# Second block's mixer: attention in small pieces between weight chunks, heads in pairs, four banks in place of two

## The chip, the cores and the metric

The program runs on one core of a Trainium2 chip. The metric is the device time of one execution, in microseconds (us), and each kernel is told by the median of its runs. A profile is one execution of it, recorded instruction by instruction. TensorE (PE) does the matmuls, VectorE (DVE), ScalarE (ACT) and GpSimd (POOL) the rest, and SyncE (SP) issues the loads of the weights.

## The reference

Two transformer blocks of two layers each, on 256 tokens of width 1024, in float32. The change touches the mixer of the second block, which is computed twice (once per layer):

```
(qa, ckv, iq, ik, iw, qs, ks, vs, cb, cc, ch, ga, gb, gc) = split(x @ w_in)
# branch a: 8 heads; an indexer picks the 64 best keys of each query, latent attention on them
score = sum_h iw_h * relu(iq_h . ik);  idx = top_k(causal(score), 64)
logits = (q_h @ w_uk_h) . ckv + bias(t - s);  p = softmax(logits on idx);  y_a = (p @ ckv) @ w_uv
# branch b: stick breaking, 8 heads of width 64
z = qs . ks / 8 ;  A[t,s] = sig(z_ts) * prod_{s<j<t} (1 - sig(z_tj)), s < t ;  y_b = A @ vs
# branch c
y_c = cb * causal_depthwise_conv3(cc * ch)
merged = sum_j sigmoid(gate_j) * (y_j @ w_branch_j);   return merged @ w_out
```

## The kernel before

All weights, some 455 MB, stream once through the core in a fixed list of chunks. A WIDE chunk is 128 x 2048 values, a HALF chunk 128 x 1024. Each goes through a ring of four slots (`RING = 4`): SP loads `raw`, ACT rounds it into `w_hi` (`split_hi`, L434), DVE subtracts to get the rest, `w_lo` (`split_lo`, L438), and PE multiplies both parts with both parts of the activations: three matmuls for one (`mm3`, `tokens`), 48 matmuls of 256 columns for a WIDE chunk in `two_tiles` (L500 to L502), 24 for a HALF one. ACT and DVE split chunk c+4 when PE has finished chunk c; `ahead.to(n)` means "split up to chunk n now", at that place of the engine's own order. The results of a chunk go to one of four PSUM banks (`acc`), and ACT or DVE must empty the bank before PE's fourth chunk from there. The other four banks are `stat`, `bc` and the two of `aux`.

Every engine's order is written by hand, as one program per engine with semaphores between them; a waiting instruction holds up all that stands behind it on its engine. In a mixer of the second block (`mix2`, twice) the chunks are numbered from `c0`: c0 to c0+4 give vs, iq, ckv, ik and iw, c0+5 to c0+16 twelve WIDE chunks, then twelve pairs of a `gate` (WIDE) and a `branch` (HALF) up to c0+40, then w_out. Between them PE does the attention, in float32, and mostly in the two banks of `aux`:

- behind c0+6: the eight heads' indexer products (`dots`, L818 and L819), each bank emptied by an ACT relu (L1275) before PE may use it again, then the turning of ckv (L825);
- behind c0+7: `q @ w_uk` (L836), in two rounds, the second after ACT has copied the first (L1289);
- behind c0+14: six blocks of logits (L849, L853). DVE takes each with its bias (L1866, L1870). Before that DVE has done the eight rounds of the top 64 (L1846, L1848), on both blocks of queries in turn, and POOL has masked the penalty;
- behind c0+17 (gate 0): 24 transposes of the probabilities (`turn`, L865), after maxima, exponentials and division of the block (DVE L1877 to L1887, ACT L1308); then p @ ckv (L924, L928), later times w_uv (L934);
- from gate 2 on, the eight stick-breaking heads, one per chunk: `z` (L876, L877) in `aux`, then ACT |z|, exp and ln (L1352 to L1356), DVE (L1925), POOL's mask (L2041), then `arg` in `stat` or `bc`: the same product once more (L889, L890) and three matmuls with triangles onto it (L891 to L893), ACT exp (L1362), POOL's mask, and `weigh` (L900, L901), which ACT and DVE split into `branches` (L1367, L1930).

Of the kernel before, what the change touches and what calls it, by code (L numbers as in the profile page):

```python
# [6 lines left out]
F32 = mybir.dt.float32  # L7
# [97 lines left out]
def pack2(i, out):  # L105

    w = {k[:-2]: v for k, v in i.items() if k.endswith("_2")}
    for l in range(LAYERS):
        for f in range(2):
            if f:  # L110
# [8 lines left out]
                out[WIDE] += [moving(vs), moving(iq), wide(qa), conv, wide(qs), wide(ks),  # L119
# [128 lines left out]
def program(nc, t):  # L248
# [11 lines left out]
    with ExitStack() as ctx:  # L260
# [52 lines left out]
        flips = (stat, bc)  # L313

# [58 lines left out]
        R = lambda n: gates[:, 12 + 2 * (n % 2):14 + 2 * (n % 2)].rearrange("p a b -> p (a b)")[:, 0:384]  # L373
# [6 lines left out]
        AW = lambda n: gates[:, 16 + 2 * (n % 2):18 + 2 * (n % 2)].rearrange("p a b -> p (a b)")[:, 0:384]  # L380
        GT = lambda n: tmp[:, 16 + 2 * (n % 2):18 + 2 * (n % 2)]
# [115 lines left out]
        def _(pe):  # L497
# [295 lines left out]
            def mix2(s, l):  # L793
# [10 lines left out]
                two_tiles(c0 + 5, t0 + 6, 8, x_hi, x_lo)  # L804

                pe.wait_ge(e["ik_rows"], 4 * (l + 1))
                pe.wait_ge(e["iq_ready"], 2 * (l + 1))
                for tt in range(2):
                    last = nc.tensor.transpose(aux[:, 0, tt * P:(tt + 1) * P], IKT[:, tt].rearrange("p d c -> p (d c)"), ident[:, :])
                last.then_inc(e["ik_turned"], 1)  # L810
                two_tiles(c0 + 6, t0 + 7, 8, x_hi, x_lo)

                pe.wait_ge(e["ik_ready"], l + 1)
                for h in range(8):
                    if h >= 2:
                        pe.wait_ge(e["dots_relu"], 8 * l + h - 1)
                    r = slice(64 * (h % 2), 64 * (h % 2) + 64)
                    nc.tensor.matmul(aux[:, h % 2, 0:P], IQ[r, h // 2, 0:P], IK[r, 0:P], start=True, stop=True)  # L818
                    nc.tensor.matmul(aux[:, h % 2, P:3 * P], IQ[r, h // 2, P:S], IK[r, :], start=True,  # L819
                                     stop=True).then_inc(e["dots_done"], 1)  # L820

                pe.wait_ge(e["ck_ready"], l + 1)
# [4 lines left out]
                two_tiles(c0 + 7, t0 + 8, 8, x_hi, x_lo)  # L827
                for q in (5, 6):
                    emptied(pe, t0 + q + 1)
                pe.wait_ge(e["ckf_ready"], l + 1)  # L830
                for h in range(8):
                    r = slice(64 * (h % 2), 64 * (h % 2) + 64)
                    if h in (4, 5):
                        pe.wait_ge(e["lat_ready"], 4 * l + h - 3)

                    last = nc.tensor.matmul(aux[:, h % 2, (h // 2 % 2) * S:(h // 2 % 2 + 1) * S], UK[r, (h // 2) * P:(h // 2 + 1) * P],  # L836
                                            QA[r, h // 2], start=True, stop=True)
                    if h % 4 >= 2:
                        last.then_inc(e["lat_done"], 1)
                for j in range(8, 15):  # L840
                    two_tiles(c0 + j, t0 + j + 1, 8, x_hi, x_lo)

                pe.wait_ge(e["lat_ready"], 4 * (l + 1))
                for n in range(6):
                    if n >= 2:
                        pe.wait_ge(e["log_taken"], 6 * l + n - 1)
                    if n < 4:
                        for hh in range(2):
                            last = nc.tensor.matmul(aux[:, n % 2, hh * S:(hh + 1) * S], QL[:, 2 * n + hh, P:S], CKF[:, :],  # L849
                                                    start=True, stop=True)  # L850
                    else:
                        for hh in range(4):
                            last = nc.tensor.matmul(aux[:, n % 2, hh * P:(hh + 1) * P], QL[:, 4 * (n - 4) + hh, 0:P],  # L853
                                                    CKF[:, 0:P], start=True, stop=True)
                    last.then_inc(e["log_done"], 1)
                for j in (15, 16):
                    two_tiles(c0 + j, t0 + j + 1, 8, x_hi, x_lo)

                def turn(n):

                    pe.wait_ge(e["turned_copied" if n >= 2 else "log_taken"], 6 * l + n - 1 if n >= 2 else 6 * (l + 1))
# [6 lines left out]
                def z(h):  # L868
                    if h == 0:
                        for q in range(13, 17):  # L870
                            emptied(pe, t0 + q + 1)
                        pe.wait_ge(e["ya_parts"], 2 * (l + 1))
                    if h >= 2:
                        pe.wait_ge(e["sp_ready"], 8 * l + h - 1)
                    r = slice(64 * (h % 2), 64 * (h % 2) + 64)
                    nc.tensor.matmul(aux[:, h % 2, 0:S], KS[r, h // 2, 0:P], QS[r, h // 2, :], start=True, stop=True)  # L876
                    nc.tensor.matmul(aux[:, h % 2, S:384], KS[r, h // 2, P:S], QS[r, h // 2, P:S], start=True,  # L877
                                     stop=True).then_inc(e["z_done"], 1)

                def arg(h):  # L880

                    out = (stat, bc)[h % 2]
                    if h >= 2:
                        pe.wait_ge(e["yb_parts"], 8 * l + h - 1)
# [1249 lines left out]
```

## Time and profile before

| what | us |
|---|---|
| runs | 2693.92, 2693.96, 2688.5 |
| median | 2693.92 |
| the profiled execution | 2687.6 |
| its span (first to last instruction) | 2685.9 |
| PE busy | 2559.0 (95%) |
| DVE busy | 1520.0 (57%) |
| ACT busy | 1240.6 (46%) |
| one mixer, from the start of c0+5 to the first matmuls of c0+41 | 263.74 |
| the same in the second layer | 263.71 |

The profiled execution lies 6.3 us under the median. 1.7 us lie around its span. In the trace a float32 matmul has two records, so that "x8" of such a line are four matmuls of the program; a weight chunk's matmuls (L500 to L502) and a transpose have one each. A matmul's duration runs until its results are there, and the next one starts before that: what a piece costs is read from start to start.

### The profile page before, as it was taken

The page shows a single profiled execution, that of the slowest core. Times are in us where ns is not written, and L with a number is a line of the kernel's source. Part 1 is how long each engine was busy: PE and PEld are TensorE (multiplying, and loading weights), DVE is VectorE, ACT ScalarE, POOL GpSimd, SP SyncE. Part 2 cuts the span into 40 slices and gives each one's busy share as a digit, 9 for nine tenths or more (in the row PEclk, how much of TensorE's full clock was granted, in tenths as well). Part 3 has the DMA queues.
Part 4 walks back from the last instruction along what each step waited for, and adds up shares of the span by engine and source line. Part 5 has one row for each costly group of instructions (what it writes and reads, how often), then busy time and mean ns, then how long its engine had stood idle before and what let it go on. Part 6 is the DMA issues. An engine that isn't in the chain of part 4 may idle for free.

```text
span 2685.9 us, 33010 instructions
## 1 busy us (share of the span) xinstructions
PE 2559.0 (95%) x13936; PEld 2203.0 (82%) x13936; DVE 1520.0 (57%) x1532; ACT 1240.6 (46%) x1354; POOL 88.1 (3%) x137
## 2 busy tenths in 40 slices
PE   7999899999998999999999899899999998999998
PEld 6888888888888878887889788788888887798787
DVE  5556865555468765464556437654655564365654
ACT  4435544444456544344353654444444434744442
POOL 0000300000002100000000000000000000100000
PEclk9999999999999999999999899999999988999999
DMA  7545345455453355565443235454555532353542
GB/s 271 183 166 212 118 149 196 173 182 211 173 200 136 143 179 182 185 221 190 176 169 116 92 136 189 165 205 173 206 187 184 188 111 79 111 188 141 217 175 94
DMA packets 68561, 454.88 MB, mean 169 GB/s; under 512 B 7568, under 2 KB 9744, under 8 KB 17600
## 3 DMA queue, kind: packets, MB, share of 16 engines
q1 hardware_dynamic: 62784, 432.18, 44.4%
q0 software_dynamic: 3552, 17.98, 1.9%
q10 hardware_dynamic: 2080, 2.62, 0.3%
q8 instruction: 111, 1.82, 0.3%
q14 instruction: 34, 0.28, 0.0%
HBM read 450.13 MB, written 2.62 MB: 169 GB/s over the span
## 4 chain that ended last, share of the span: by engine, by line
PE 81%; DVE 8%; ACT 7%; issue 4%; DMA 0%; POOL 0%; DVEq 0%; SPq 0%; ACTq 0%; POOLq 0%
PE acc L532 20%; PE acc L534 20%; PE acc L533 20%; PE acc L500 5%; PE acc L502 5%; PE acc L501 5%; ACT w_hi L434 4%; DVE w_lo L438 2%; PE aux L601 1%; DVE tmp L1680 1%; PE stat L548 0%; DVE tmp L1691 0%; PE bc L548 0%; DMA raw<-in_w 0%; PE aux L1005 0%
## 5 line engine op out<-in xcount | busy, mean ns | idle before, releaser
L438 DVE TENSOR_TENSOR w_lo<-raw,w_hi 128x2048 fp32r<-128x2048 f32 (+1 forms) x430 | 940.5, 2190 | 854.5 <-ACT w_hi L434 851.9
L434 ACT ACTIVATE w_hi<-raw 128x2048 fp32r<-128x2048 f32 (+1 forms) x430 | 786.2, 1832 | 636.0 <-PE acc L534 580.0
L532 PE MATMUL acc<-w_hi,x_hi 128*128 128x512 f32 (+1 forms) x1664 | 653.6, 393 | 20.8 <-DVE x_lo L1492 11.7
L534 PE MATMUL acc<-w_lo,x_hi 128*128 128x512 f32 (+1 forms) x1664 | 647.3, 389 | 0.0
L533 PE MATMUL acc<-w_hi,x_lo 128*128 128x512 f32 (+1 forms) x1664 | 646.8, 389 | 0.0
L532 PEld LDWEIGHTS acc<-w_hi,x_hi 128*128 128x128 f32 x1664 | 314.6, 189 | 88.7 <-issue 14.3
L534 PEld LDWEIGHTS acc<-w_lo,x_hi 128*128 128x128 f32 x1664 | 314.2, 189 | 65.2
L533 PEld LDWEIGHTS acc<-w_hi,x_lo 128*128 128x128 f32 x1664 | 314.8, 189 | 62.2
L500 PE MATMUL acc<-x_hi,w_hi 128*128 128x256 f32 x1216 | 352.4, 290 | 0.0
L501 PE MATMUL acc<-x_lo,w_hi 128*128 128x256 f32 x1216 | 347.4, 286 | 0.0
L502 PE MATMUL acc<-x_hi,w_lo 128*128 128x256 f32 x1216 | 347.0, 285 | 0.0
L532 PE MATMUL acc<-w_hi,h_parts 128*128 128x512 f32 x704 | 275.2, 391 | 0.0
L534 PE MATMUL acc<-w_lo,h_parts 128*128 128x512 f32 x704 | 274.1, 389 | 0.0
L533 PE MATMUL acc<-w_hi,h_parts 128*128 128x512 f32 x704 | 274.0, 389 | 0.0
L500 PEld LDWEIGHTS acc<-x_hi,w_hi 128*128 128x128 f32 x1216 | 237.1, 195 | 3.5 <-issue 1.9
L501 PEld LDWEIGHTS acc<-x_lo,w_hi 128*128 128x128 f32 x1216 | 236.9, 195 | 0.7 <-issue 0.5
L502 PEld LDWEIGHTS acc<-x_hi,w_lo 128*128 128x128 f32 x1216 | 236.7, 195 | 0.0
L534 PEld LDWEIGHTS acc<-w_lo,h_parts 128*128 128x128 f32 x704 | 132.2, 188 | 27.5
L532 PEld LDWEIGHTS acc<-w_hi,h_parts 128*128 128x128 f32 x704 | 132.2, 188 | 27.0
L533 PEld LDWEIGHTS acc<-w_hi,h_parts 128*128 128x128 f32 x704 | 132.2, 188 | 27.0
L500 PE MATMUL acc<-branches,w_hi 128*128 128x256 f32 x384 | 110.9, 289 | 0.0
L1075 ACT ACTIVATE tmp<-acc 128x512 f32<-128x512 f32 (+1 forms) x96 | 54.0, 563 | 121.7 <-PE acc L534 121.6
(335 smaller groups left out, 2377.6 us busy)
## 6 DMA issues: line engine op xcount, KB each, us to landing
raw<-in_w SPq DMA_DIRECT2D x388, 1024.0 KB, 4.8
raw<-in_w SPq DMA_DIRECT2D x40, 512.0 KB, 3.2
tmp<-in_norm_gb POOLq DMA_DIRECT2D x8, 1024.0 KB, 5.2
tmp<-in_norm_gb POOLq DMA_DIRECT2D x7, 512.0 KB, 4.0
gates<-in_mixc POOLq DMA_DIRECT2D x2, 800.0 KB, 4.6
raw<-in_w SPq DMA_DIRECT2D x2, 800.0 KB, 4.4
skew<-tmp ACTq DMA_DIRECT2D x1, 1536.0 KB, 6.6
small<-in_small POOLq DMA_DIRECT2D x2, 722.0 KB, 6.5
```

The source lines that it names most:

```text
L434: nc.scalar.activation(w_hi[:, slot, 0:kind], raw[:, slot, 0:kind], ACT.Copy).then_inc(hi_done, 1)
L438: nc.vector.tensor_tensor(w_lo[:, slot, 0:kind], raw[:, slot, 0:kind], w_hi[:, slot, 0:kind].bitcast(F32), ALU.subtract).then_inc(lo_done, 1)
L500: nc.tensor.matmul(out, w_hi_, v_hi_, start=start, stop=False)
L501: nc.tensor.matmul(out, w_hi_, v_lo_, start=False, stop=False)
L502: return nc.tensor.matmul(out, w_lo_, v_hi_, start=False, stop=stop)
L532: nc.tensor.matmul(out, vh, wh, start=first and k == 0, stop=False)
L533: nc.tensor.matmul(out, vl, wh, start=False, stop=False)
L534: last = nc.tensor.matmul(out, vh, wl, start=False, stop=last_k and k == nk - 1)
L601: last = nc.tensor.transpose(aux[:, tt, q * P:(q + 1) * P], HID[:, tt, q * P:(q + 1) * P], ident[:, :])
L1075: nc.scalar.activation(SIL[:, tt, 0:w], ps(tile)[:, 0:w], ACT.Silu)\
L1680: V_.tensor_tensor(flat(EB(n)).rearrange("p (g w) -> p g w", w=w), bb, bb[:, :, w // 2 - 1:w // 2].to_broadcast([P, 2 * S // w, w]), ALU.s ...
```

## The change

1. The weight list is reordered: the convolution's first three chunks (cc, ch, cb of the first half) come before qa, and qs and ks come by halves in turn (qs0, ks0, qs1, ks1). The number and size of chunks stays.
2. `four` names the four banks beside `acc`. Dots, latents and logits use all four. Dots come as heads 0 to 3 behind c0+6 and 4 to 7 behind c0+7; the latents behind c0+9 and c0+10; the logits behind c0+10 (one block), c0+11 (three), c0+12 and c0+13 (one each); `z` of the first pair behind c0+15, the turns as 2+2+2 behind c0+16, gate 0 and branch 0; p @ ckv as 2+2.
3. The relu's results `R` get four buffers in `tmp` in place of two in `gates`.
4. The top 64 are found for the first block of queries in full (`top(0, 8)`) before the second's (3+3+2 rounds), and penalty, maxima, exponentials and division follow for each block apart.
5. Stick-breaking goes by four pairs of heads. `z` of both heads is computed at once into two banks and stays there; `arg` adds the triangle matmuls onto it and no longer repeats the product. ACT's exp and ln, POOL's masks and the split of the result take a pair at once. The pairs are at gates 0 to 7 instead of one head per chunk from gate 2 on.

The diff, cut to its core:

```
-                out[WIDE] += [moving(vs), moving(iq), wide(qa), conv, wide(qs), wide(ks),
+                qs, ks = wide(qs), wide(ks)
+                out[WIDE] += [moving(vs), moving(iq), conv[:3], wide(qa), conv[3:], qs[:1], ks[:1], qs[1:], ks[1:],
...
+        four = (aux[:, 0, :], aux[:, 1, :], stat[:, :], bc[:, :])
+        LOGITS = ((4, 0), (5, 1), (0, 2), (1, 3), (2, 0), (3, 1))
+        STICKS = ((2, 3), (2, 3), (0, 1), (2, 3))
...
-        R = lambda n: gates[:, 12 + 2 * (n % 2):14 + 2 * (n % 2)].rearrange("p a b -> p (a b)")[:, 0:384]
+        R = lambda n: tmp[:, 28 + 2 * (n % 4):30 + 2 * (n % 4)].rearrange("p a b -> p (a b)")[:, 0:384]
...  PE
+                def dots(h):
+                    if h >= 4:
+                        pe.wait_ge(e["dots_relu"], 8 * l + h - 3)
...
+                for h in range(4):
+                    dots(h)
+                two_tiles(c0 + 7, t0 + 8, 8, x_hi, x_lo)
+                for h in range(4, 8):
+                    dots(h)
+                two_tiles(c0 + 8, t0 + 9, 8, x_hi, x_lo)
...
+                latent(0)
+                latent(1)
+                two_tiles(c0 + 10, t0 + 11, 8, x_hi, x_lo)
+                latent(2)
+                latent(3)
+                logits(0)
+                two_tiles(c0 + 11, t0 + 12, 8, x_hi, x_lo)
+                for k in (1, 2, 3):
+                    logits(k)
...
+                def arg(p):
+                    pe.wait_ge(e["sp_masked"], 4 * l + p + 1)
+                    for h in range(2):
+                        out, sp = four[STICKS[p][h]], SP(h)
+                        nc.tensor.matmul(out[:, 0:S], NTRI, sp[:, 0:S], start=False, stop=False, **kw)
+                        nc.tensor.matmul(out[:, P:S], NONE_, sp[:, S:384], start=False, stop=False, **kw)
+                        last = nc.tensor.matmul(out[:, S:384], NTRI, sp[:, S:384], start=False, stop=True, **kw)
+                    last.then_inc(e["arg_done"], 1)
...
+                z(0)
+                two_tiles(c0 + 16, t0 + 17, 8, x_hi, x_lo)
+                turn(0)
+                turn(1)
+                gate(0)
+                arg(0)
+                turn(2)
+                turn(3)
+                branch(0, lambda k: pe.wait_ge(e["conv_parts"], 2 * l + k // 2 + 1))
...
+                z(1)
+                branch(2)
+                gate(3)
+                arg(1)
+                z(2)
...  ACT
+                    for h in range(2):
+                        ac(nc.scalar.activation(SP(h), four[STICKS[p][h]][:, 0:384], ACT.Abs))
+                    ac.settle()
+                    ac(nc.scalar.activation(SPP, SPP, ACT.Exp, scale=-1.0))
+                    ac.settle()
+                    nc.scalar.activation(SPP, SPP, ACT.Ln, bias=1.0).then_inc(e["zl_ready"], 1)
...
+                exps(0)
+                ahead.to(c0 + 16)
...
+                exps(1)
+                take(c0 + 15, t0 + 16, QS[:, 2:4], 0.125)
+                ahead.to(c0 + 19)
+                soft(0)
...  DVE
+                top(0, 8)
+                penalty(0)
...
+                maxima(1)
+                ahead.to(c0 + 18)
+                ahead.to(c0 + 19)
+                divided(1)
+                soft(0)
...  POOL
-                for h in range(8):
...
+                for p in range(4):
+                    pool.wait_ge(e["sp_ready"], 4 * l + p + 1)
+                    strict(SPP, e["sp_masked"])
+                    pool.wait_ge(e["a_exp"], 4 * l + p + 1)
+                    strict(AWP, e["a_masked"])
```

How it moves the instructions, as each engine gets them. On PE, at the logits, before (`tmp` holds q's latents and ckv; L500 to L502 are a chunk's matmuls):

```order
L502 MATMUL acc<-x_hi,w_lo 128x256
L849 MATMUL aux<-tmp 128x256 x8
L853 MATMUL aux<-tmp 128x128 x8
L500 MATMUL acc<-x_hi,w_hi 128x256
L501 MATMUL acc<-x_lo,w_hi 128x256
L502 MATMUL acc<-x_hi,w_lo 128x256
```

and of the new kernel the three blocks that now stand behind c0+11 (L510 to L512 are the chunk's matmuls there, L864 and L860 the two forms of a block of logits):

```order
L510 MATMUL acc<-x_hi,w_hi 128x256
L511 MATMUL acc<-x_lo,w_hi 128x256
L512 MATMUL acc<-x_hi,w_lo 128x256
L864 MATMUL aux<-tmp 128x128 x4
L860 MATMUL stat<-tmp 128x256 x2
L860 MATMUL bc<-tmp 128x256 x2
L510 MATMUL acc<-x_hi,w_hi 128x256
```

The six blocks stood in a row in two banks; now three are in three banks, and the others between other chunks.

On PE, at one stick-breaking head before (`gates` holds q, k and the softplus, `small` the triangles):

```order
L502 MATMUL acc<-x_hi,w_lo 128x256
L876 MATMUL aux<-gates 128x256
L877 MATMUL aux<-gates 128x128
L889 MATMUL stat<-gates 128x256
L890 MATMUL stat<-gates 128x128
L891 MATMUL stat<-gates,small 128x256
L892 MATMUL stat<-gates,small 128x128
L893 MATMUL stat<-gates,small 128x128
L500 MATMUL acc<-branches,w_hi 128x256
```

and `arg` of the first pair behind gate 0 in the new kernel:

```order
L511 MATMUL acc<-x_lo,w_hi 128x256
L512 MATMUL acc<-x_hi,w_lo 128x256
L944 MATMUL stat<-gates,small 128x256
L945 MATMUL stat<-gates,small 128x128
L946 MATMUL stat<-gates,small 128x128
L944 MATMUL bc<-gates,small 128x256
L945 MATMUL bc<-gates,small 128x128
L946 MATMUL bc<-gates,small 128x128
L896 MATMUL aux<-ident,tmp 128x128 x8
```

The second product of q and k (L889, L890) has gone, and eight turns follow.

On DVE, ahead of `arg` of the first pair in the new kernel (L448 is `w_lo`, L1967 takes a block of logits, L1981 to L1985 are the maxima of the second block, L1992 its division, L1997 and L1998 the pair's softplus):

```order
L1967 TENSOR_TENSOR tmp<-aux,tmp 128x512
L1981 TENSOR_TENSOR tmp<-tmp 128x2048
L1983 TENSOR_REDUCE sm<-tmp 128x8
L1985 TENSOR_SCALAR sm<-sm 128x8
L448 TENSOR_TENSOR w_lo<-raw,w_hi 128x1024
L448 TENSOR_TENSOR w_lo<-raw,w_hi 128x2048
L1990 RECIPROCAL sm<-sm 128x8
L1992 TENSOR_TENSOR tmp<-tmp,sm 128x2048
L1997 SCALAR_TENSOR_TENSOR gates<-stat,gates 128x384
L1998 SCALAR_TENSOR_TENSOR gates<-bc,gates 128x384
```

The pair's softplus now stands behind the second block's softmax and the splits of c0+18 and c0+19, where before its first head came behind branch 1.

## Rows read from the trace of the kernel before

**Rows 1.** The page: the span, PE's busy time, the chain that ended last.

```profile
span 2685.9 us, 33010 instructions
PE 2559.0 (95%) x13936; PEld 2203.0 (82%) x13936; DVE 1520.0 (57%) x1532; ACT 1240.6 (46%) x1354; POOL 88.1 (3%) x137
PE 81%; DVE 8%; ACT 7%; issue 4%; DMA 0%; POOL 0%; DVEq 0%; SPq 0%; ACTq 0%; POOLq 0%
```

**Rows 2.** PE's waits in the first mixer: total us, times, longest us.

```profile
PE bc L889 <- DVE branches L1930: 5.5, 3, 2.4
PE aux L849 <- DVE tmp L1866: 5.3, 1, 5.3
PE aux L865 <- DVE tmp L1887: 3.1, 1, 3.1
```

**Rows 3.** Stretches: from:to, us, PE busy (records), granted clock, DMA share, GB/s.

```profile
1375.22:1638.96 263.74, 239.90 (x1735) 0.94 0.38 135
2133.61:2397.32 263.71, 239.87 (x1735) 0.94 0.37 135
...
1408.32:1448.74 40.42, 40.42 (x338) 1.00 0.37 131
1448.74:1461.94 13.20, 7.86 (x34) 0.74 0.36 119
...
1479.46:1490.64 11.18, 5.37 (x26) 0.59 0.17 57
...
1494.06:1499.05 4.99, 4.99 (x14) 1.00 0.28 82
...
1505.30:1507.18 1.88, 1.88 (x18) 1.00 0.00 0
...
1512.53:1518.48 5.95, 5.95 (x50) 1.00 0.58 233
1535.49:1538.22 2.73, 2.73 (x20) 1.00 0.00 0
```

**Rows 4.** PE in order: start, us, instruction. Dots of heads 0 and 1.

```profile
1387.12 0.50 PE L818 MATMUL aux<-tmp 64*128 64x128 f32 x4
1387.44 0.61 PE L819 MATMUL aux<-tmp 64*128 64x256 f32 x4
```

**Rows 5.** PE in order: first round of latents, first two blocks of logits, eight transposes.

```profile
1403.74 1.14 PE L836 MATMUL aux<-tmp,small 64*128 64x256 f32 x8
...
1448.74 1.89 PE L849 MATMUL aux<-tmp 128*128 128x256 f32 x8
...
1374.43 1.04 PE L658 MATMUL aux<-ident,tmp 128*128 128x128 f32 x8
```

**Rows 6.** PE in order: z, arg and weigh at the fourth chunk of the heads.

```profile
1535.49 0.48 PE L876 MATMUL aux<-gates 64*128 64x256 f32 x1
1535.50 0.48 PE L889 MATMUL stat<-gates 64*128 64x256 f32 x1
...
1536.35 0.70 PE L891 MATMUL stat<-gates,small 128*128 128x256 f32 x2
...
1537.42 0.65 PE L900 MATMUL bc<-gates 128*64 128x256 f32 x2
```

**Rows 7.** DVE and ACT in the mixer, by line: us in total, mean ns, idle before.

```profile
L438 DVE TENSOR_TENSOR w_lo<-raw,w_hi 128x2048 fp32r<-128x2048 f32 x26 | 59.5, 2291 | 74.1 <-ACT w_hi L434 74.0
L434 ACT ACTIVATE w_hi<-raw 128x2048 fp32r<-128x2048 f32 x25 | 47.7, 1908 | 16.4 <-PE acc L502 16.4
L1354 ACT ACTIVATE gates<-gates 128x384 f32<-128x384 f32 x8 | 4.2, 525 | 0.3
L1356 ACT ACT_TABLE_LOAD x8 | 10.3, 1283 | 0.1
L1308 ACT ACTIVATE tmp<-tmp,sm 128x256 f32<-128x256 f32 x8 | 4.0, 494 | 0.3 <-DVE sm L1881 0.3
L1848 DVE MATCH_REPLACE8 tmp<-sm,tmp 128x256 f32<-128x256 f32 x8 | 3.3, 409 | 0.0
```

More of the change, by code:

```diff
@@ L866, in turn @@
                     last.then_inc(e["turned"], 1)
[L868 to L878, printed above, removed]
@@ L915, in mix2, with value_latents @@
[L915 to L919 removed]
+                def value_latents(n):
                     if n >= 2:
@@ L955, in mix2, with values @@
-                step(8)
-                weigh(7)
-                for q in range(9, 12):
-                    step(q)
+                def values():
+                    pe.wait_ge(e["ol_ready"], 4 * (l + 1))
+                    for h in range(8):
+                        out = aux[64 * (h % 2):64 * (h % 2) + 64, h // 4, (h // 2 % 2) * S:(h // 2 % 2 + 1) * S]
+                        last = nc.tensor.matmul(out, UV[:, 64 * h:64 * h + 64], OL[:, h], start=True, stop=True)
+                        if h % 4 == 3:
+                            last.then_inc(e["ya_done"], 1)
@@ new lines, in weigh @@
+                def weigh(p):
+                    pe.wait_ge(e["a_masked"], 4 * l + p + 1)
+                    for h in range(2):
+                        out = four[STICKS[p][0]][64 * h:64 * h + 64, :]
+                        at = 64 * (2 * p + h)
+                        v = [flat(VS[:, 2 * tt:2 * tt + 2])[:, at:at + 64] for tt in range(2)]
+                        nc.tensor.matmul(out[:, 0:S], v[0], AW(h)[:, 0:S], start=True, stop=False, **kw)
+                        last = nc.tensor.matmul(out[:, P:S], v[1], AW(h)[:, S:384], start=False, stop=True, **kw)
+                    last.then_inc(e["yb_done"], 1)
@@ new lines, in mix2 @@
+                gate(2)
+                values()
+                z(1)
[3 more added lines that the diff above has]
+                z(2)
+                branch(3)
+                gate(4)
+                weigh(1)
+                arg(2)
+                branch(4, lambda k: pe.wait_ge(e["ya_parts"], 2 * l + k // 2 + 1))
+                gate(5)
+                weigh(2)
+                z(3)
+                branch(5)
+                gate(6)
+                arg(3)
@@ L1369, in step @@
[L1369 to L1384 removed]
+                gate_next(2)
@@ new lines, in mix2 @@
+                soft(1)
+                branch(2)
+                gate(3)
+                weights(1)
+                gate_next(3)
+                soft(2)
+                branch(3)
+                gate(4)
+                heads_high(1)
+                weights(2)
+                gate_next(4)
+                branch(4)
+                gate(5)
+                heads_high(2)
+                gate_next(5)
+                soft(3)
+                branch(5)
+                gate(6)
+                weights(3)
@@ L1916, in mix2 @@
                 gate(1)
+                heads_low(0)
+                branch(1)
+                gate(2)
                 for n in range(2):
```

523 lines of the change are left out of this document (276 added, 247 removed).

## The prediction

> **What bounds the kernel now.** I read the page first. PE is busy 95% of the span, no other engine above 57%, and the chain that ended last is 81% PE [rows 1]. So a change pays only where it takes matmuls away from PE, or time in which PE waits or runs at the lower of its two clock levels. I then looked for such time in the two mixers that the change touches. The stretch from c0+5 to the first matmuls of c0+41 takes 263.74 us, of which PE is busy 239.90, and in the second layer 263.71 and 239.87 [rows 3]: 23.8 us of waiting in each, the same in both, so one mixer is worked out and doubled. The granted clock there is 0.94 of full, which is some 32 us at 1.2 GHz in place of 2.4, and it is low exactly where PE waits: 0.74 at the logits, 0.59 at the turns, 1.00 in seven unbroken chunks [rows 3]. The list of waits names the hand-overs: a head's `arg` for the split of the head two before (5.5 us), the third block of logits for the bank that DVE has not yet taken (5.3), the turns for the division (3.1) [rows 2]. All come from two things: two banks for a chain of many links, and a chain that PE reaches before the other engines are done with it. DMA is at 0.38 of its time in the stretch and PE waits for no chunk there [rows 2, 3], so there is room for a faster PE.
>
> **What the change makes of PE's time.** The chunks stay: 24 WIDE and 12 HALF ones, and at the end of the stretch twelve matmuls of c0+41. Seven chunks in a row take 40.42 us, 5.77 each; one between two pieces of attention takes 5.95 [rows 3]. Nearly all are between pieces after the change, the last eight not: 24 at 5.9 is 141.6, 12 halves at 3.0 is 36.0, the twelve double-width matmuls 2.9. Together 180.5 us.
>
> To this come the pieces, each at the price that a row shows at the full clock, read from start to start:
> - dots: two heads take 0.93 us [rows 4]; four such are 3.7. The four single transposes about them, at 0.1 each, 0.4.
> - latents: four matmuls take 1.14 where rows 0 to 63 and 64 to 127 alternate [rows 5]. Now two of one half of the array come before two of the other, so less of it overlaps: between 1.1 and 1.9, I take 1.3, twice 2.6.
> - logits: two blocks take 1.89 [rows 5], six 5.7.
> - turns: eight transposes take 0.8 (to the chunk that starts at 1375.22) [rows 3, 5], 24 take 2.4.
> - p @ ckv 4.99, and w_uv 1.88 [rows 3].
> - heads: at the fourth chunk of the heads `z` of one head and the repeated product of another ran at once in the two halves of the array, 10 ns apart; both were done in 0.86 us (1535.49 to 1536.35) [rows 6]. A pair's `z` is the same four matmuls: 4 x 0.86 = 3.4. The three triangle matmuls took 1.07 a head (to 1537.42): 8.6 for eight. `weigh` took 0.80 for one head (to the stretch's end at 1538.22) [rows 3, 6]. A pair's two heads write different halves of the columns and overlap only in the middle: between 0.8 and 1.6, I take 1.2, which is 4.8 for four.
>
> The pieces sum to 38.5, with the chunks 219.0 us. Against 263.7 this is 44.7 less: 23.8 of waits, and 20.9 of busy time. Some 8 of these are the heads (`z`, the repeated product, `arg` and `weigh` of eight heads at full clock took about 25, now 16.8); the rest is the time at 1.2 GHz, which goes with the waits that caused it.
>
> A rule speaks against many small pieces. A chunk between pieces takes 0.18 us more than one in a run [rows 3]. The Trainium skill (TensorEngine Tiling (Array Packing), Tiling Modes, Key Properties) says that a change of the tiling mode drains the engine; the pieces of 64 rows or 64 columns among chunks of 128 are such changes. The trace agrees with at most this price, and the sum above has it in the 5.9.
>
> **Where new waits could stand.** I walked the four engines' new orders from the start of c0+5, with the rows' durations. PE reaches c0+9 at 27.6 us, c0+11 at 42.5, c0+13 at 57.9, c0+15 at 70.5, c0+16 at 77.2, gate 0 at 84, its end at 89.7.
> - The second round of dots comes a chunk after the first, and the first's relus take 4 x 0.5: no wait. Of the logits, three blocks have three free banks; the fourth and fifth wait for additions done at 47 and 56, asked for at 57 and 64.
> - DVE is the engine that the change loads most in this part. A split of a chunk costs it 2.29 [rows 7]. Between c0+9 and c0+19 it does eight rounds on either block (a round on the wide block is a maximum and a replacement, 0.41 each [rows 7], and a short load between, about 0.95), the logits, maxima and divisions (a 2048-wide operation takes as long as a split, 2.29), both convolutions and the splits. Its order gives: `w_lo` of c0+13 at 41, of c0+15 at 56, c0+16 at 66, c0+17 at 72, c0+18 at 78, c0+19 at 86. PE asks at 58, 71, 77, 84, 94, 98. The leads are 17, 15, 11, 12, 16 and 12 us. Behind `exps(0)` (8 x 0.39, ACT) the split `w_hi` of c0+16 (1.91) waits, and behind it DVE's; this is in the 11.
> - The tightest place is `arg` of the first pair. The second block's maxima end at 77 on DVE; then ACT has eight exponentials at 0.49, a copy, the split of c0+19 (1.91) and `soft(0)` (two |z|, exp and ln of 768 columns, between 0.53 for 384 and 1.91 for 2048, I take 0.86, and a table load of 1.28) [rows 7]: 88. DVE's softplus of both heads ends at 89.7, POOL's two masks at 90.7. PE is there at 89.7: a wait of 1.0. Queued behind `arg` are the turns 2 and 3 and branch 0, all of PE.
> - The second pair's mask is ready at 130, PE is there at 131; third 142 and 144; fourth 165 and 166. No wait, but leads of 1 to 2 us. They are this short since ACT's soft stands behind a split each time; ACT has eight table loads of 1.28 less than before [rows 7], since ln comes once for a pair.
>
> **The sum.** 44.7 less the 1.0 is 43.7 a mixer, 87.4 for both. From the profiled execution's own 2687.6 this gives 2600.2 us; the median of the runs lies 6.3 above that execution, so I forecast **2606 us**. Ends of the unknown prices: `weigh` at 0.8 and 1.6, latents at 1.1 and 1.9, chunks at 5.77 and 5.95, the wait at 0 and 3, move a mixer by about 5 down and 5 up: 2596 to 2617.
>
> **Rivals.**
> 1. *The clock stays low in places, or the tight masks are late.* Each head's mask is on a chain over three engines with 1 us of lead; a hand-over of 0.1 more at each of its eight links takes that away. For it: about waits of 3 us the turns' stretch fell to 0.59 [rows 2, 3], so a wait costs more than itself. If a third to a half of the old loss remains (0.06 of 264 is 16 us, so 5 to 8), with waits of 1 to 3 us, a mixer gives back 6 to 13: 2618 to 2632. Against: the pieces are now short, 0.8 to 2.9 us, between chunks of 5.8. In a sentence of its own: the Trainium skill (TensorE: Matmul & The Clock Gate, Part 4: PE-mode transpose) says transposes don't count as busy for the clock; the eight that precede 1375.22 ran at full clock between chunks [rows 5], and the turns are now in eights, so by the rows this costs nothing.
> 2. *The supply of chunks falls behind.* DVE needs more than the 11 us of lead about c0+16, as the top-k rounds and softmax wait for ACT in turn (maxima, exps, `w_hi`, `w_lo`). Then PE waits for `w_lo`, and every us past the lead is one on PE. At 10 to 25 us a mixer: 2626 to 2656.
> 3. *Slower than before.* The same coupling, complete: `w_hi` of c0+15 waits for c0+11, DVE's maxima stand behind `w_lo` of c0+15, and ACT's next splits behind the exponentials. If none of top-k (13), logits (4), maxima (7), divisions (4), exponentials (7) and convolution (6) were hidden by chunks, that is 41 us of PE waiting, and at the clock of the turns (0.59) some 15 more: 56 a mixer, 12 above the gain of 44, twice 12 above 2694: 2718. It decides from 44 us a mixer on, four times the smallest lead. Against it: before, DVE did the top-k rounds beside chunks and PE waited for none of its splits [rows 2].
> 4. *Nothing gained*: waits of just the size of the gain. It needs the same as 3, less of it: 2689 to 2699.
>
> **Chances.** The forecast's case (2596 to 2617) 0.62; rival 1 0.22; rival 2 and what lies between it and no change 0.11; rival 4 0.02; rival 3 0.03. The range must leave out no more than 2 in 10: it goes from 2592 (the lower end, less the spread of the runs) to 2634, which takes in rival 1 and the near end of rival 2. Faster by over 0.2% (5.4 us, about what a measurement of this kernel can tell from no change) has 0.95, within it 0.02, slower 0.03.
>
> **What would show it.** In the new profile the stretch from c0+5 to c0+41 should take about 220 us, with PE's waits under 3 us in total and the granted clock near 0.99. The list of waits should have no `acc` matmul that waits for `w_lo`; if it does, rival 2 is at work. A wait of the triangle matmuls for POOL of about 1 us behind gate 0 would show the walk right; one in each pair, rival 1. The pair's `z` should have four matmuls in 0.86 us and the turns ten a microsecond. Wrong would be the forecast if the banks of a pair or of the logits are not free when PE comes, or if parts outside the two mixers move.

## The result and the profile after

The changed kernel took 2584.83 us (median of 4 runs, 2582.8 to 2586.8) and the kernel before, run beside it, 2693.44 (4 runs, 2688.5 to 2693.96). The ratio is 0.9601, with a 95% interval of 0.9584 to 0.9617. The forecast was 2606, with a range from 2592 to 2634: the direction and the mechanism hold, but the gain is 108.6 us where 87.4 was worked out, and the time lies below the whole range.

The page of the changed kernel: the span, PE and DVE, and the chain that ended last.

```profile
span 2581.1 us, 32824 instructions
PE 2502.9 (97%) x13872; PEld 2165.6 (84%) x13872; DVE 1515.5 (59%) x1526; ACT 1210.1 (47%) x1314; POOL 87.9 (3%) x105
...
PE 83%; DVE 7%; ACT 5%; issue 4%; DMA 0%; POOL 0%; DVEq 0%; SPq 0%; ACTq 0%; POOLq 0%
```

Against [rows 1] the span is 104.8 us shorter and PE has 56.1 us less to do. PE is still the bound, at 97%, and DVE is no nearer to it than before in any way that the chain shows. Now the stretches, with the columns of [rows 3]: from and to, us, PE busy (records), granted clock, DMA share, GB/s. The first two are the two mixers from c0+5 to the first matmuls of c0+41; the third is what lies between them but for the last 0.9 us, the fourth what follows the second.

```profile
1375.02:1587.82 212.80, 212.32 (x1703) 1.00 0.45 167
2083.88:2296.68 212.80, 212.33 (x1703) 1.00 0.46 167
1587.82:2083.00 495.18, 484.03 (x2301) 0.99 0.49 181
2296.68:2581.10 284.42, 265.45 (x1288) 0.98 0.43 157
```

A mixer went from 263.74 to 212.80 us, and the other from 263.71 to 212.80: 50.9 less in each, 101.8 in all. The other 3.0 us of the span's 104.8 lie outside: 0.2 ahead of the first mixer, 4.2 behind the second (288.58 before, 284.42 now), less 1.4 between them (494.65 to 496.06). The code there is the same in both kernels, and the records show 43.9 us at 1.2 GHz there before and 40.3 after, in other places.

Within a mixer the 50.9 fall into three parts. PE's waits went from 23.8 us to 0.5 (23.4 less). In the kernel before, the records show 34.1 us of each mixer at 1.2 GHz, of which PE was busy 27.4, so that the same work at 2.4 GHz saves 13.7; after, the granted clock is 1.00 from end to end. The rest of the busy time, some 13.9 us, is a remainder that was not measured piece by piece: matmuls that are gone (the repeated product, 32 records a mixer), matmuls that now run beside others, and ends of matmuls that no longer stand ahead of a wait, where they count as busy. PE's list of waits for the first mixer of the changed kernel (what PE waited for: total us, times, longest us) has one line:

```profile
PE stat L944 <- POOLq L2198: 0.5, 1, 0.5
```

That is the triangle matmul of the first pair behind gate 0, which waits for POOL's masks: the one wait that the prediction had named, at 1.0 us.

### The profile page after: what moved, and what is told of

It is laid out like the page before. It is cut to its first block, busy times and chain, and to the rows that moved or that the text cites. A ratio compares the mean times of both kernels' runs of the same rounds, so it can differ in the third digit from the quotient of the medians.

```text
span 2581.1 us, 32824 instructions
## 1 busy us (share of the span) xinstructions
PE 2502.9 (97%) x13872; PEld 2165.6 (84%) x13872; DVE 1515.5 (59%) x1526; ACT 1210.1 (47%) x1314; POOL 87.9 (3%) x105
## 4 chain that ended last, share of the span: by engine, by line
PE 83%; DVE 7%; ACT 5%; issue 4%; DMA 0%; POOL 0%; DVEq 0%; SPq 0%; ACTq 0%; POOLq 0%
PE acc L542 21%; PE acc L544 21%; PE acc L543 21%; PE acc L510 5%; PE acc L511 5%; PE acc L512 5%; ACT w_hi L444 3%; DVE w_lo L448 2%; PE aux L611 1%; DVE tmp L1787 1%; ACT tmp L1342 1%; PE stat L558 0%; DVE tmp L1798 0%; PE bc L558 0%; DMA raw<-in_w 0%
## 5 line engine op out<-in xcount | busy, mean ns | idle before, releaser
L448 DVE TENSOR_TENSOR w_lo<-raw,w_hi 128x2048 fp32r<-128x2048 f32 (+1 forms) x430 | 941.1, 2191 | 836.6 <-ACT w_hi L444 834.2
L510 PE MATMUL acc<-x_hi,w_hi 128*128 128x256 f32 x1216 | 350.4, 288 | 0.0
L512 PE MATMUL acc<-x_hi,w_lo 128*128 128x256 f32 x1216 | 344.6, 283 | 0.0
L510 PEld LDWEIGHTS acc<-x_hi,w_hi 128*128 128x128 f32 x1216 | 233.7, 192 | 3.1 <-issue 2.5
L512 PEld LDWEIGHTS acc<-x_hi,w_lo 128*128 128x128 f32 x1216 | 233.6, 192 | 0.0
L510 PE MATMUL acc<-branches,w_hi 128*128 128x256 f32 x384 | 111.2, 290 | 0.0
```

Of the source, the lines that this page charges most:

```text
L448: nc.vector.tensor_tensor(w_lo[:, slot, 0:kind], raw[:, slot, 0:kind], w_hi[:, slot, 0:kind].bitcast(F32), ALU.subtract).then_inc(lo_done, 1)
L510: nc.tensor.matmul(out, w_hi_, v_hi_, start=start, stop=False)
L512: return nc.tensor.matmul(out, w_lo_, v_hi_, start=False, stop=stop)
```

## The experiments

Eight kernels were run in two groups, each group beside runs of the kernel before: median 2688.8 us in the first (e1, e2, e4, e6), 2692.26 in the second. The changed kernel itself was run in neither, so "above the changed kernel" compares medians of different groups, between which the kernel before alone moved by up to 4.6 us; the lengths of the mixers in the traces are the surer measure. The theory is that PE bounds the mixers from end to end, that the waits were those of too few banks and of pieces too close to each other, and that the clock follows the waits. The rivals each say that some part of the change isn't needed. No run puts back the waits at the turns (3.1 and 2.7 us before) or among the heads (5.5, 1.4 and 1.1), which were over half of the 23.8 us a mixer: that they went is seen in the trace, but which part of the change took them away was not tried.

**e1: the repeated product put back.** The pair's `z` is computed a second time ahead of `arg`.

```diff
                 def arg(p):
                     pe.wait_ge(e["sp_masked"], 4 * l + p + 1)
+                    rows = (slice(0, 64), slice(64, 128))
+                    for h in range(2):
+                        nc.tensor.matmul(four[STICKS[p][h]][:, 0:S], KS[rows[h], p, 0:P], QS[rows[h], p, :],
+                                         start=True, stop=True, **kw)
...
                     for h in range(2):
                         out, sp = four[STICKS[p][h]], SP(h)
```

> The new kernel, with the product of q and k repeated in each pair's arg (four matmuls more a pair, the two heads side by side, 32 in the two mixers). Theory (PE's own matmuls are the bound there, and their price is the spacing of starts): a pair's z takes 0.85 us from start to start in the new kernel's trace, so 4 x 0.85 x 2 = 6.8 us more, 2584.8 to 2591.6. If pieces cost as much as I put them at before (with the tail of the last matmul), 8 to 9 us more. Rival (the heads' chain over ACT, DVE and POOL is the bound among the gates): under 2 us more.

It took 2591.19 us (2590.11 to 2591.74), 6.4 above the changed kernel; ratio to before 0.9634 [0.9619, 0.9648]. Its two mixers:

```profile
1375.38:1592.00 216.62, 216.13 (x1735) 1.00 0.46 164
2087.36:2303.99 216.63, 216.16 (x1735) 1.00 0.46 164
```

Each is 3.8 us longer, all of it PE's busy time, 0.95 a pair where 0.85 was expected. What is added to PE here is paid in full, so the chain over ACT, DVE and POOL isn't the bound among the gates; how near it is, an addition to PE can't tell, since it gives the others more time. The product as pairs is worth some 7 us in the two mixers. In the kernel before, its eight repeats ran one by one, four of them beside another head's `z` and four alone, and what it cost there was not measured.

**e2: dots and logits on two banks again.** The places of the pieces stay as in the change.

```diff
-        LOGITS = ((4, 0), (5, 1), (0, 2), (1, 3), (2, 0), (3, 1))
+        LOGITS = ((4, 0), (5, 1), (0, 0), (1, 1), (2, 0), (3, 1))
...
                 def dots(h):
-                    if h >= 4:
-                        pe.wait_ge(e["dots_relu"], 8 * l + h - 3)
+                    if h >= 2:
+                        pe.wait_ge(e["dots_relu"], 8 * l + h - 1)
...
-                    if k >= 4:
-                        pe.wait_ge(e["log_taken"], 6 * l + k - 3)
+                    if k >= 2:
+                        pe.wait_ge(e["log_taken"], 6 * l + k - 1)
...
```

> The new kernel with dots and logits in two banks again, at the new places: a head's dots wait for the relu two heads before, a block of logits for the addition two blocks before. Theory (the four banks take the waits away): waits of PE at L825 of 0.5 to 1 us a head, and of 4 to 5 us at the logits behind c0+11, where the fourth block waits for an addition that DVE does only behind the convolution; with the clock 9 to 15 us a mixer, 2603 to 2615 in all. Rival (the spreading between chunks did it, banks matter little): under 3 us a mixer, below 2591.

It took 2602.3 us (2602.11 to 2603.69), 17.5 above the changed kernel; ratio 0.9677 [0.9661, 0.9693]. That is just under the low end of what was expected. PE's waits in its first mixer, then both mixers and the first round of dots:

```profile
PE aux L860 <- DVE tmp L1971: 6.3, 1, 6.3
PE aux L824 <- ACT tmp L1326: 1.1, 2, 0.6
```

```profile
1375.48:1598.00 222.52, 215.11 (x1703) 0.98 0.44 159
2093.08:2316.75 223.67, 216.25 (x1703) 0.98 0.45 158
1387.38:1390.11 2.73, 2.16 (x18) 1.00 0.91 315
```

The mixers are 9.7 and 10.9 us longer. The large wait is at the fourth block of logits, the last of the three behind c0+11, for the bank of the second, which DVE takes only at 1432.90, behind its top-64 rounds, the convolution and a split; it is longer than I had said (4 to 5). The dots wait 1.1 us in all, less than I had said, but each round takes 2.73 us where the changed kernel takes 1.62, so they cost 2.2 a mixer: the ends of matmuls ahead of a wait count as busy. The waits are 6.9 us more than in the changed kernel, and the busy time is 2.8 (first mixer) and 3.9 (second) more. Of that some 1.1 is the dots' ends; the records show 6.8 and 10.2 us at 1.2 GHz, in which PE was busy 3.6 and 6.2, so the low clock makes up 1.8 and 3.1. The banks count most at the logits; at the dots two of them cost 2.2 us a mixer even with a chunk between the rounds.

**e3: the dots in one row, on four banks.** The eight dots follow each other, as in the kernel before; DVE's and ACT's orders go along.

```diff
                 for h in range(4):
                     dots(h)
-                two_tiles(c0 + 7, t0 + 8, 8, x_hi, x_lo)
                 for h in range(4, 8):
                     dots(h)
+                two_tiles(c0 + 7, t0 + 8, 8, x_hi, x_lo)
```

> The new kernel with the eight heads' dots in one row behind c0+6 in four banks, ACT's relus and DVE's scores in a row too, and DVE's first convolution behind the scores. Theory (four banks are enough where ACT is free): the first relu is done before PE has issued head 3, no wait over 0.5 us, one seam less: 2583 to 2587, the same as the new kernel. Rival (the pieces must be apart): waits of 1 to 3 us at the dots and a clock below 1 behind them, 2588 to 2596.

It took 2584.91 us (2582.6 to 2591.54); ratio 0.9608 [0.959, 0.9627], no different from the changed kernel. Its mixers:

```profile
1380.64:1593.58 212.94, 212.45 (x1703) 1.00 0.46 167
2088.94:2301.86 212.92, 212.44 (x1703) 1.00 0.47 167
```

They are 0.1 us longer each, and PE doesn't wait at the dots. So with four banks the distance isn't needed here; e6 shows that this hangs on ACT being free when the dots come. The first mixer begins 5.6 us later than in the changed kernel although all code ahead of it is the same: there the records show 34.1 us at half speed where the changed kernel has 17.1. This is where single executions differ, and why the mixers are compared by their own length here.

**e4: a wait put in.** The fifth and sixth blocks of logits wait for the additions to the fourth.

```diff
                     if k >= 4:
-                        pe.wait_ge(e["log_taken"], 6 * l + k - 3)
+                        pe.wait_ge(e["log_taken"], 6 * l + 4)
```

> The new kernel with one wait put in: the fifth block of logits (behind c0+12) waits until DVE has taken the fourth, 3.6 us later than PE comes there by the new kernel's trace (1431.2 to 1434.8). Theory (a wait costs more than itself, since the clock falls to 1.2 GHz behind it): 3.6 and 1.7 to 3.4 more a mixer, 10.6 to 14 us in all, 2595 to 2599, with a granted clock under 1 in the stretch. Rival (one wait by itself leaves the clock): 7.2 us, 2592. Second rival (later waits absorb it): under 3 us.

It took 2594.75 us (2593.29 to 2595.12), 9.9 above the changed kernel; ratio 0.9646 [0.9632, 0.9661]. The wait in its first mixer, and both mixers:

```profile
PE aux L860 <- DVE tmp L1967: 3.6, 1, 3.6
```

```profile
1375.07:1593.34 218.27, 214.69 (x1703) 0.98 0.45 162
2088.78:2304.65 215.87, 212.29 (x1703) 1.00 0.46 164
```

The same 3.6 us wait stands in both mixers, and half a microsecond of it comes back, since the masks are then ready in time. In the second mixer this is all: 3.1 us longer. In the first the clock fell within the wait, at 1433.42, for 6.8 us at 1.2 GHz, which cost another 2.4 us of busy time. So a wait can cost more than itself, but the same wait did so in one mixer of two: both the theory (which had it in both) and the rival (in none) are half right.

**e5: `z` head after head.** The second half's matmul of the first head is issued before the first one of the second head.

```diff
                     for h in range(2):
                         nc.tensor.matmul(four[STICKS[p][h]][:, 0:S], KS[rows[h], p, 0:P], QS[rows[h], p, :],
                                          start=True, stop=True, **kw)
-                    for h in range(2):
                         last = nc.tensor.matmul(four[STICKS[p][h]][:, S:384], KS[rows[h], p, P:S], QS[rows[h], p, P:S],
                                                 start=False, stop=True, **kw)
```

> The new kernel with z of a pair issued one head after the other (both matmuls of the first, then both of the second). Theory (matmuls on different halves of the rows overlap only as neighbours): a pair's z goes from 0.85 to about 1.3 us, 3.6 us in all, 2588.4. Rival (the order of issue doesn't matter): within 1 us of 2584.8.

It took 2584.86 us (2582.0 to 2587.69); ratio 0.9608 [0.9592, 0.9624]. The first mixer is 212.84 us long, so that nothing was lost. The theory that a pair needs alternating issue falls. In the program PE gets `stat` 256, `stat` 128, `bc` 256, `bc` 128 columns, in this order; PE in the order in which it ran them (start, us, instruction), with the row of the next chunk as the end:

```profile
1450.84 0.48 PE L933 MATMUL stat<-gates 64*128 64x256 f32 x1
1450.85 0.48 PE L933 MATMUL bc<-gates 64*128 64x256 f32 x1
...
1451.38 0.27 PE L935 MATMUL stat<-gates 64*128 64x128 f32 x1
1451.39 0.27 PE L935 MATMUL bc<-gates 64*128 64x128 f32 x1
...
1451.70 0.39 PE L510 MATMUL acc<-x_hi,w_hi 128*128 128x256 f32 x1
```

The second head's matmul, third in the program, starts 10 ns after the first, and the four are done in 0.86 us, against 0.85 in the changed kernel. The one that stands between them in the order holds it up by nothing that can be seen.

**e6: the kernel before with the dots alone on four banks.**

The relu gets four result buffers too.

```diff
...
                 for h in range(8):
-                    if h >= 2:
-                        pe.wait_ge(e["dots_relu"], 8 * l + h - 1)
+                    if h >= 4:
+                        pe.wait_ge(e["dots_relu"], 8 * l + h - 3)
                     r = slice(64 * (h % 2), 64 * (h % 2) + 64)
-                    nc.tensor.matmul(aux[:, h % 2, 0:P], IQ[r, h // 2, 0:P], IK[r, 0:P], start=True, stop=True)
+                    nc.tensor.matmul(four[h % 4][:, 0:P], IQ[r, h // 2, 0:P], IK[r, 0:P], start=True, stop=True)
...
```

> The kernel before with one part of the change alone: dots in four banks with four result buffers, still eight heads in a row behind c0+6. Theory: the waits among the dots fall from 2.9 us to about 1.2 (the first relu still stands behind ACT's split of a chunk), the piece from 9 us to 5, and the half-speed time behind it goes: 5 to 7 us a mixer, 2693.4 to 2680 to 2684. Rival (what matters is that the second four heads come a chunk later): under 2 us a mixer, 2690 or more.

It took 2684.3 us (9 runs, 2678.86 to 2687.31); ratio 0.9972 [0.9961, 0.9982], a gain of 0.3%. The eight dots, then both mixers, then the stretch from the latents on:

```profile
1388.12:1395.07 6.95, 3.92 (x35) 1.00 0.43 163
1376.22:1639.90 263.68, 239.65 (x1735) 0.94 0.38 135
2134.93:2394.98 260.05, 236.02 (x1735) 0.95 0.38 137
1400.99:1450.00 49.01, 47.10 (x359) 0.93 0.36 128
```

The same in the kernel before: the eight dots with the turning of ckv, and the chunk behind them.

```profile
1387.12:1396.44 9.32, 6.45 (x36) 0.80 0.27 106
1396.44:1403.74 7.30, 7.30 (x51) 0.79 0.41 144
```

The dots take 6.95 us where the kernel before takes 9.32, and run at the full clock. But the first mixer as a whole is as long as before (263.68 against 263.74), and the second 3.7 shorter. I had said 5 to 7 in each, with the dots' waits down from 2.9 us to 1.2. They did not go down. PE's waits at the dots and at the turning of ckv, first in the kernel before, then in e6:

```profile
PE aux L818 <- ACT gates L1275: 2.2, 2, 2.0
PE aux L825 <- ACT gates L1275: 0.7, 1, 0.7
...
PE aux L826 <- ACT tmp L1276: 1.8, 1, 1.8
PE aux L819 <- ACT tmp L1276: 1.3, 1, 1.3
```

They are 2.9 us before and 3.1 now: PE gets through four heads in place of two and then waits all the same. The 1.3 us are for ACT's first relus. In e6 they stand behind the split of a chunk; in e3, with the same eight dots on the same four banks, ACT has been idle when the dots come (start, us, instruction; e6, then e3):

```profile
1388.73 1.90 ACT L435 ACTIVATE w_hi<-raw 128x2048 fp32r<-128x2048 f32 x1
1390.53 0.86 ACT L1276 ACTIVATE tmp<-aux 128x384 f32<-128x384 f32 x2
...
1393.50 0.87 ACT L1326 ACTIVATE tmp<-aux 128x384 f32<-128x384 f32 x2 [4.14 <-PE aux L825]
```

In ACT's order before, the result of c0+6 is copied and a chunk split ahead of the relus; in the new order, which the reordered weight list makes possible, neither stands there. The 1.8 us are for the last relus, since the turning of ckv stands right behind the dots; in e3 and in the changed kernel it comes later. So four banks without the new orders take none of the waits away. This is read from the traces and the code; the orders were not tried alone. What e6 gained lies in the clock. All waits of its first mixer are 24.0 us, as before (23.8), and so is the time at 1.2 GHz (34.1); it only lies elsewhere, for the latents' stretch had 1.00 and has 0.93 here. In the second mixer the same 24.0 us of waits go with 27.3 us at 1.2 GHz in place of 34.1.

**e7: the last part of the mixer crosswise.** The list of waits of the changed kernel over its whole span has, among larger ones, these two lines:

```profile
PE acc L542 <- DVE x_lo L1874: 9.2, 2, 4.6
PE acc L542 <- DVE merged L2068: 4.8, 2, 2.4
```

Both stand in `skewed_out`, the last product of a mixer, which multiplies chunk j = 0, then chunk j = 1 for each half n of the output; the second chunk needs inputs that DVE is still making. For the first half of the tokens e7 takes the first chunk of both output halves before the second of either. This is no part of the change, but a further step.

```diff
                 for tt in range(2):
-                    for n in range(2):
-                        for j in range(each):
+                    nj = [(0, 0), (1, 0), (0, 1), (1, 1)] if each == 2 and tt == 0 else [(n, j) for n in range(2) for j in range(each)]
+                    for n, j in nj:
+                        if True:
```

> The new kernel with another order in the last product of every mixer (first and second block): for the first half of the tokens the first chunk of both output halves, then the second of both, so that 2.7 us of matmuls stand between the need for the first and for the last part of the merged branches. Theory (the waits left at these places, 2.4 us twice for merged L2068 and 4.6 us twice for x_lo L1874, are plain waits of PE): 2.4 and 2.7 less at each, 10 us in all, 2574.5. Rival (the same chain ends later elsewhere, in the norm behind it): under 3 us less, 2582 or more.

It took 2571.74 us (2569.29 to 2572.57), 13.1 less than the changed kernel; ratio to before 0.9554 [0.954, 0.9568]. In its list of waits the line of `merged` is gone and that of `x_lo` is down from 9.2 to 3.7 in all:

```profile
PE acc L542 <- DVE x_lo L1875: 3.7, 2, 1.9
```

10.3 us of waits went, as expected; the rest of the 13.1 was not taken apart. The profiled execution shows 26.8 us at 1.2 GHz over its span where the changed kernel's shows 40.3, but e3 shows that such a difference can lie between single executions. This version is faster than both kernels.

**e8: e7, with the first pair's `arg` behind branch 0.** It asks whether the wait of 0.5 us for POOL is worth moving.

```diff
                 gate(0)
-                arg(0)
                 turn(2)
                 turn(3)
                 branch(0, lambda k: pe.wait_ge(e["conv_parts"], 2 * l + k // 2 + 1))
+                arg(0)
                 turn(4)
```

> As e7_out_crosswise, and the first pair's arg behind branch 0 in place of before it, 3 us later. Theory: the wait of 0.5 us for POOL goes, and nothing else waits, since the weights of that pair are asked for a gate later: 1 us less than e7_out_crosswise, 2573.5. Rival (arg_done is late for ACT, whose in-order queue has the turned probabilities behind the exponential): a wait at the turns or at weigh, 1 to 4 us more than e7_out_crosswise.

It took 2571.11 us (2570.55 to 2574.82); ratio 0.9556 [0.9542, 0.957], the same as e7. Its first mixer has no wait for POOL, but another:

```profile
PE aux L897 <- ACT tmp L1376: 1.8, 1, 1.8
...
1368.17:1582.00 213.83, 212.06 (x1703) 1.00 0.47 165
```

The turns, reached earlier, now wait for ACT, as the rival said, and the mixer is 213.83 us long where e7's is 212.80. The total shows neither gain nor loss: 1.0 us a mixer is no more than the runs of one kernel differ by.

## Why the prediction was wrong in size and right in kind

**What held.** The walk over the four engines' orders, made from durations of the kernel before, met the new trace closely. `arg` of the first pair was to be reached 89.7 us after the start of c0+5 and its masks to be ready at 90.7; PE was there at 88.7 and the masks came at 89.2 (1464.25 less 1375.02). The splits of the chunks had leads of 11 us and more by the walk, and no `acc` matmul waits for `w_lo`: rivals 2 to 4, all of them a late supply, did not come. The later pairs, with leads of 1 to 2 us, did not wait (the new trace has leads of 1.3 to 1.7), and the clock stayed at 1.00, so rival 1 did not either. What it would have cost e4 shows: of a wait of 3.6 us, 3.1 are back in the mixer's length, and 5.5 where the clock fell. One reading ahead of the sum doesn't hold: the prediction put all waits down to two banks and to PE coming too early, and at the dots e6 shows four banks alone to take no wait away.

On the rule that was weighed for rival 1, transposes ran in eights between other work and the granted clock of the whole mixer is 1.00. By the Trainium skill (TensorE: Matmul & The Clock Gate, Part 4: PE-mode transpose) they don't count as busy for the clock in the way other matmuls do; no run here has transposes without other matmuls close by, so this case neither bears it out nor speaks against it.

**The step that failed** is the price list of the pieces, 38.5 us "each at the price that a row shows at the full clock, read from start to start". They were not what a piece costs between chunks, in two ways. Dots, latents and logits were read where a wait followed the piece (for the logits it is the 5.3 us of [rows 2]), so up to the end of the last matmul; in the new kernel the next piece starts before that end. And `arg`'s 1.07 was read up to the start of a piece of another shape, with the seam between them, which two heads in a row now have once. These are the rows of the changed kernel (start, us, instruction): three blocks of logits (the first of four heads' 128 columns, the others of two heads' 256) and the chunk behind them; the first pair's `arg`, with the turns behind it; and one pair's `weigh`.

```profile
1422.83 1.06 PE L864 MATMUL aux<-tmp 128*128 128x128 f32 x8
1423.72 1.03 PE L860 MATMUL stat<-tmp 128*128 128x256 f32 x4
1424.58 1.03 PE L860 MATMUL bc<-tmp 128*128 128x256 f32 x4
1425.26 0.47 PE L510 MATMUL acc<-x_hi,w_hi 128*128 128x256 f32 x1
...
1464.25 0.70 PE L944 MATMUL stat<-gates,small 128*128 128x256 f32 x2 [0.48 <-POOLq L2198]
...
1465.23 0.60 PE L944 MATMUL bc<-gates,small 128*128 128x256 f32 x2
...
1466.11 1.04 PE L896 MATMUL aux<-ident,tmp 128*128 128x128 f32 x8
...
1476.56 0.66 PE L956 MATMUL stat<-gates 128*64 128x256 f32 x4
...
1477.04 0.40 PE L957 MATMUL stat<-gates 128*64 128x128 f32 x4
1477.37 0.70 PE L904 MATMUL aux<-tmp 128*128 128x512 f32 x1
```

A block of logits lasts 1.03 us, but the next starts after 0.86 and the chunk after 0.68; I had 0.945, half of the 1.89 in [rows 5], with a tail in it. The second head's triangle matmuls take 0.88 (1465.23 to 1466.11), where I had 1.07. And the seam towards a chunk was in the 5.9 for a chunk already, so part of it was counted twice. The stretches of four pieces and of chunks between pieces (columns as above): four heads' dots, the chunk behind the logits, two chunks in a row (c0+14 and c0+15), a pair's `z`, the first pair's `arg`, a pair's `weigh`.

```profile
1386.91:1388.53 1.62, 1.62 (x18) 1.00 0.84 238
...
1425.26:1431.20 5.94, 5.94 (x50) 1.00 0.00 0
1438.50:1450.29 11.79, 11.79 (x99) 1.00 0.36 135
1450.29:1451.14 0.85, 0.85 (x9) 1.00 0.00 0
1464.25:1466.11 1.86, 1.86 (x13) 1.00 0.04 9
1476.56:1477.37 0.81, 0.81 (x10) 1.00 0.88 339
```

Term by term, for the first mixer, predicted and measured in us (measured from start to start, all pieces of a kind together):

| term | predicted | measured | too much |
|---|---|---|---|
| chunks | 180.5 | 179.5 | 1.0 |
| `weigh` | 4.8 | 3.2 | 1.6 |
| `arg` | 8.6 | 7.2 | 1.4 |
| logits | 5.7 | 4.7 | 1.0 |
| dots | 3.7 | 3.2 | 0.5 |
| latents | 2.6 | 2.1 | 0.5 |
| p @ ckv | 5.0 | 4.5 | 0.5 |
| `z` | 3.4 | 3.4 | 0 |
| wait for POOL | 1.0 | 0.5 | 0.5 |

That is 7.0 of the 7.2 us by which 43.7 falls short of 50.9. Only `z`, whose row had the same matmuls in the same company and ended where the next piece started, was exact. For p @ ckv the first round takes 1.42 us (1.86 before, where the second round followed it) and the second 3.03 (3.13). The half chunk behind the first round takes 3.27 us where the one behind two turns takes 2.95, so some 0.3 of it has only moved into the term of the chunks.

**Two of the terms have another cause.** For `weigh` I took 1.2 a pair, since "a pair's two heads write different halves of the columns and overlap only in the middle", and for the latents 1.3, since two of one half of the array come before two of the other. They took 0.81 and 1.07: one head's price in [rows 6] for two heads, and no more than the 1.14 of the alternating order in [rows 5]. Both rest on a loss of overlap that no row had shown: the two heads' `weigh` overlap in full, and that the order must alternate is false for the latents and, by e5, for `z`. For these two my low ends (0.8 and 1.1) were right. For dots, logits, `arg` and p @ ckv the prediction gave no ends at all, which is why the range's floor held only 5 us a mixer where 7.2 was needed; the low ends that it does give sum to 6.1, not to 5. Two other figures of it don't come out either, though nothing hangs on them: rival 1's upper end of 13 a mixer is 11 by its own terms (8 and 3), and ACT has seven table loads fewer in a mixer, not eight (17 before, 10 now).

**The rest of the distance.** From 2606 to 2584.8 are some 21.7 us before rounding: 14.4 from the mixers, 3.0 from the code outside them, which I had taken as unmoved, and 4.3 from the step from the profiled execution to the median. I had added 6.3 us, what the kernel before showed; the changed kernel's median lies 2.0 above its profiled execution. The 6.3 was no fixed step: all 23 runs of the kernel before lie either at 2687.5 to 2688.9 (11 of them) or at 2692.3 to 2694.1 (12), the profiled execution was of the lower group and the median of the upper. Of the 3.0 outside nothing is caused by the change that the records show: the clock's falls lie elsewhere, as they do from one execution to the next in e3. Its cause stays open beyond that.

**The clock's share.** The prediction had put 20.9 us of busy time as some 8 for the heads and the rest for the clock. Measured, it is 27.6, of it 13.7 for the clock. That figure is worked out from the half-speed time of the kernel before; no run removed the low clock and left the waits. What e4 and e6 add is that the clock's loss isn't in proportion to the waits: the same wait of 3.6 us had it in one mixer and not in the other, and in e6 the same 24.0 us of waits went with 34.1 us at 1.2 GHz in one mixer and 27.3 in the other.

## What to carry to other kernels

Where an engine is to be filled without gaps, price each piece from its start to the start of what follows it, in a place where nothing is waited for; a piece followed by a wait has its tail in its price, and a seam that is in the neighbour's price must not be in its own too. Give every price an end on either side, and not only those that are plainly unknown: here four small terms that seemed read off, each 11 to 21% too high, made 3.4 of the 7.2 us, and two that were guessed 2.1. And before a wait is put down to too few banks, see what the engine that empties them does first: in e6 more banks moved PE's wait to other heads and took nothing away, since ACT was at a split when the first results came.

## What the runs showed of the hardware

Two matmuls on different halves of the array (rows 0 to 63 and 64 to 127) start together even if a further one on the first half stands between them in the program: 10 ns apart in e5, the four matmuls in 0.86 us, and in 0.85 in alternating order. Two heads' `weigh` on different halves of the columns took 0.81, where one head took 0.80. The Trainium skill (TensorEngine Tiling (Array Packing), Tiling Modes, Key Properties) says that different tiles can execute in parallel; the trace agrees, and in e5 the order of issue of the four made no difference.

The clock's fall within a wait of 3.6 us came in one mixer of e4 and not in the other, though the program around was the same in both; when it came it lasted 6.8 us at 1.2 GHz.
